# Who subtracts the expert weights: from VectorE and GpSimd in turn to VectorE alone, with the output copy on ScalarE

## The chip, the cores and the metric

The kernel runs on one core of a Trainium2 chip. The metric is the device time of one execution in microseconds. A core has TensorE (PE in the profile), VectorE (DVE), ScalarE (ACT), GpSimd (POOL) and SyncE (SP), which here only issues DMAs. The engines run their own lists of instructions and wait for each other through semaphores.

## What is computed

A transformer block (attention, short convolution, experts, a gated embedding) and then a second one (retention, a Fourier branch, a convolutional feed-forward net), on 512 tokens of 1024 numbers in float32. The change touches the experts of the first block alone:

```python
ht = h.reshape(b * s, d)                       # 512 tokens x 1024
g_val, g_idx = lax.top_k(softmax(ht @ w_rg + b_rg), 1)       # one group of 4 experts
e_val, e_idx = lax.top_k(softmax(e_logits of that group), 2) # two experts in it
a = jnp.einsum('td,edf->tef', ht, w_gate)      # 16 experts, 1024 -> 256
u = jnp.einsum('td,edf->tef', ht, w_up)
hid = jax.nn.silu(a) * u * combine[..., None]
out = jnp.einsum('tef,efd->td', hid, w_down)   # 256 -> 1024
```

Each token goes to 2 of 16 experts: 1024 pairs of a token and an expert.

## The kernel before

**Slots and steps.** The pairs are sorted on the chip into 23 slots of at most 128 pairs: one for each of 16 experts, and 7 more for what overflows. One slot is one step `n`. A step gathers the rows of its tokens from `h_rows` in device memory into `hg` (one indirect DMA, two buffers), transposes them on TensorE, multiplies by the gate and up weights, applies SiLU and the share of the pair (`hid`), transposes `hid`, multiplies by the down weights, copies the result from PSUM to `y_sb` (one buffer) and scatters its rows to `y_rows` (one indirect DMA). Both indirect DMAs are issued by GpSimd.

**Units.** The weights of a step are three units of 1 MB: `3n-1` (gate and up, first half), `3n` (second half) and `3n+4` (down); TensorE uses the units in order of their number, so the down product of step `n-1`, unit `3n+1`, follows the second gate and up unit of step `n`. Products keep float32 precision by splitting every operand in two: ScalarE rounds the unit (`unit_hi`, line 1750), another engine subtracts that from the raw unit (`unit_lo`, line 1755), and TensorE multiplies high by high, high by low and low by high: 12 matmuls of 128x512 a unit, 36 a step. There are four raw buffers and four pairs of split buffers. SyncE loads unit `u` (two DMAs of 512 KB, line 1654) once unit `u-4` is subtracted. ScalarE rounds unit `u` once it has landed and TensorE has used unit `u-4`. Tokens (`s_hi`, `s_lo`, lines 1870 and 1908) and `hid` (`g_hi`, `g_lo`, lines 1888 and 1933) are split in the same way by ScalarE and VectorE.

**Order.** Nothing is planned at run time: each engine's order is its program. In step `n`:

- TensorE: gate and up, first half; transpose `hid` of `n-1` (line 1810); transpose the tokens of `n+1` (line 1775); gate and up, second half; down product of `n-1` (lines 1826 to 1828).
- ScalarE: SiLU (line 1882), round unit `3n+4`, round unit `3n+5`, `g_hi`, tokens of `n+2`, round unit `3n+6`.
- VectorE: `hid` (line 1926), unit `3n+4` if it is VectorE's, copy of the output of `n-1` (line 1913), unit `3n+5`, `g_lo`, tokens of `n+2`, unit `3n+6`.
- GpSimd: gather for step `n+2` (line 1700), scatter of the output of `n-1` (line 1705), unit `3n+4` (line 1755).

GpSimd subtracts the 21 down units of steps 0 to 20 (`POOL_UNITS`), VectorE the other 48. The two count in semaphores of their own, `e_plo` and `e_dlo`, and `wait_unit_lo` picks the one to wait for. The copy of the output waits for the down product of its step (`e_used`) and for the landing of the scatter before it (`e_ystore`); the down product waits for the copy before it (`e_ycopy`). Twice the stage does something else: in step 6 VectorE computes `last_pick` (into `p_lo`, line 1939), and SyncE, after the loads of step 8, waits for it and loads 1 MB of context into the same memory (`ctx_in`, line 1689).

Of the kernel before, what the change touches and what calls it, by code (L numbers as in the profile page):

```python
# [24 lines left out]
ACT = mybir.ActivationFunctionType  # L25
# [69 lines left out]
STEPS = SLOTS  # L95
UNITS = 3 * STEPS
# [66 lines left out]
def build(nc, a, const, out):  # L163
# [7 lines left out]
    with root:  # L171
# [118 lines left out]
        with ExitStack() as s:  # L290
            sb = buffers(s)
            y_sb = sb("y_sb", [P, D])
# [92 lines left out]
        psum = root.enter_context(nc.psum_tensor("psum", [P, 8, T], F32))  # L385
# [1021 lines left out]
        def copy_embedded(act, c):  # L1407
# [2 lines left out]


        E = semaphores("e_wr", "e_matched", "e_chain", "e_shift", "e_exp", "e_routed", "e_hot", "e_stored",
                       "e_hg0", "e_hg1", "e_in0", "e_in1", "e_in2", "e_in3", "e_whi", "e_dlo", "e_plo", "e_used",
                       "e_turned", "e_hi", "e_lo", "e_silu", "e_hid", "e_ycopy", "e_ystore")
        CHOSEN, PLACED, COMBINED, WEIGHED, TABLED, LAST_PICKED = 1, 2, 3, 4, 5, 6
        MATCHED, RANKED, LISTED, SHARED = KC + 1, KC + 2, KC + 3, KC + 4
# [202 lines left out]
        def unit_down(n):  # L1619
            return min(3 * n + 4, UNITS - 1)  # L1620

        POOL_UNITS = [unit_down(n) for n in range(STEPS - 2)]
        DVE_UNITS = [u for u in range(UNITS) if u not in POOL_UNITS]

        def wait_unit_lo(eng, u):
            if u in POOL_UNITS:
                eng.wait_ge(E["e_plo"], POOL_UNITS.index(u) + 1)
            else:
                eng.wait_ge(E["e_dlo"], DVE_UNITS.index(u) + 1)

        def tokens_of(s):

# [59 lines left out]
        def moe_gpsimd(pool):  # L1692
            pool.wait_ge(G["chunk_done"], 2 * (G_WO + 3) + 2)
            for j in range(2):
                pool.memset(hg[j][:, :], 0.0).then_inc(W["wm_silu"], 1)

            def gather(s):
                if s >= 2:
                    pool.wait_ge(E["e_turned"], tokens_turned(s - 2))
                pool.indirect_dma_start(hg[s % 2][:, :], None, h_rows,  # L1700
                                        bass.IndirectOffsetOnAxis(ap=at_row[:, 0, s:s + 1], axis=0),
                                        bounds_check=T - 1, oob_is_err=False).then_inc(E[f"e_hg{s % 2}"], 16)

            def store_y(s):
                pool.indirect_dma_start(y_rows, bass.IndirectOffsetOnAxis(ap=at_row[:, 1, s:s + 1], axis=0),
                                        y_sb[:, :], None, bounds_check=PAIRS - 1, oob_is_err=False)\
                    .then_inc(E["e_ystore"], 16)

            pool.wait_ge(E["e_stored"], 32)
            pool.wait_ge(E["e_routed"], PLACED)  # L1710
            pool.wait_ge(W["wm_silu"], 5)
            for s in range(2):
                gather(s)
            pool.memset(y_sb[:, :], 0.0).then_inc(W["wm_silu"], 1)
            pool.wait_ge(W["wm_silu"], 6)
            store_y(SLOTS - 1)
            for n in range(STEPS):
                if n + 2 < SLOTS:
                    gather(n + 2)
                if n:  # L1720
                    pool.wait_ge(E["e_ycopy"], n)
                    store_y(n - 1)
                if unit_down(n) in POOL_UNITS:
                    unit_lo(pool, unit_down(n))
            pool.wait_ge(E["e_ystore"], 16 * SLOTS)
            wait_unit_lo(pool, UNITS - 1)
            pool.wait_ge(E["e_turned"], tokens_turned(SLOTS - 1))
            from_rows = y_rows.rearrange("(j i p) d -> p j i d", j=TOP, p=P)
            for half in range(2):
                for j in range(TOP):  # L1730
                    pool.dma_start(y_back[:, j, :, half * T:(half + 1) * T], from_rows[:, j, :, half * T:(half + 1) * T])\
                        .then_inc(E[f"e_hg{half}"], 16)
# [8 lines left out]
        def unit_hi(act, u):  # L1741
            if u >= UNITS:
                return
            b = u % 4
            act.wait_ge(E[f"e_in{b}"], 32 * (u // 4) + 32)
            if u >= 4:
                act.wait_ge(E["e_used"], u - 3)
            elif u % 2:
                act.wait_ge(G["chunk_done"], 2 * (G_WO + 3 + u // 2) + 2)
            act.activation(u_hi[b][:, :, :], raw_of(u)[:, :, :], ACT.Copy).then_inc(E["e_whi"], 1)  # L1750

        def unit_lo(eng, u):
            b = u % 4
            eng.wait_ge(E["e_whi"], u + 1)
            eng.tensor_tensor(u_lo[b][:, :, :], raw_of(u)[:, :, :], u_hi[b][:, :, :].bitcast(F32), ALU.subtract)\  # L1755
               .then_inc(E["e_plo" if u in POOL_UNITS else "e_dlo"], 1)

        def pick_bank(c):
            return (6, 7, 0, 1, 2, 3, 6, 7)[c]
# [104 lines left out]
        def moe_scalar(act):  # L1864

            def tokens_hi(s):
                if s == 1:
                    wait_unit_lo(act, 0)
                act.wait_ge(E["e_turned"], tokens_turned(s))
                act.activation(s_hi[s % 2][:, :, :], tokens_of(s), ACT.Copy).then_inc(E["e_hi"], 1)  # L1870

            tokens_hi(0)
            unit_hi(act, 1)
            unit_hi(act, 2)
            tokens_hi(1)
            unit_hi(act, 3)
            act.wait_ge(E["e_stored"], 32)
            for n in range(STEPS):
                act.wait_ge(E["e_used"], unit_in(n, 1) + 1)
                if n >= 2:  # L1880
                    act.wait_ge(E["e_hid"], n - 1)
                act.activation(act_u[:, n % 2, :], psum[:, n % 2, 0:2 * P], ACT.Silu).then_inc(E["e_silu"], 1)
                unit_hi(act, 3 * n + 4)
                unit_hi(act, 3 * n + 5)
                act.wait_ge(E["e_turned"], hidden_turned(n))
                if n >= 2:
                    act.wait_ge(E["e_used"], unit_down(n - 2) + 1)
                act.activation(g_hi[:, n % 2, :, :], psum[:, HID_BANK + n % 2, 0:2 * P].rearrange("p (j t) -> p j t", j=2),
                               ACT.Copy).then_inc(E["e_hi"], 1)
                if n + 2 < SLOTS:  # L1890
                    tokens_hi(n + 2)
                unit_hi(act, 3 * n + 6)
            act.wait_ge(E["e_used"], UNITS)
            act.activation(flat(s_hi[(SLOTS - 2) % 2]).rearrange("p (b t) -> p b t", b=2), psum[:, Y_BANK:Y_BANK + 2, :],
                           ACT.Copy).then_inc(E["e_hi"], 1)
            split_hi(act, G_PG, G_PG % 2)
            for c in range(KC):
                square(act, R_MOE, c)

        def moe_vector(dve):  # L1900

            def dve_lo(u):
                if u in DVE_UNITS:
                    unit_lo(dve, u)

            def tokens_lo(s):
                dve.wait_ge(E["e_hi"], tokens_turned(s))
                dve.tensor_tensor(s_lo[s % 2][:, :, :], tokens_of(s), s_hi[s % 2][:, :, :].bitcast(F32), ALU.subtract).then_inc(E["e_lo"], 1)

            def copy_y(n):  # L1910
                dve.wait_ge(E["e_used"], unit_down(n) + 1)
                dve.wait_ge(E["e_ystore"], 16 * n + 16)
                dve.tensor_copy(y_sb[:, :].rearrange("p (b t) -> p b t", b=2), psum[:, Y_BANK:Y_BANK + 2, :])\
                   .then_inc(E["e_ycopy"], 1)

            tokens_lo(0)
            route_late(dve)
            dve_lo(1)
            dve_lo(2)
            tokens_lo(1)  # L1920
            dve_lo(3)
            for n in range(STEPS):
                dve.wait_ge(E["e_silu"], n + 1)
                if n >= 2:
                    dve.wait_ge(E["e_turned"], hidden_turned(n - 2))
                dve.scalar_tensor_tensor(out=hid[:, n % 2, :], in0=psum[:, n % 2, 2 * P:4 * P], scalar=comb_s[:, n:n + 1],
                                         in1=act_u[:, n % 2, :], op0=ALU.mult, op1=ALU.mult).then_inc(E["e_hid"], 1)
                dve_lo(3 * n + 4)
                if n:
                    copy_y(n - 1)  # L1930
                dve_lo(3 * n + 5)
                dve.wait_ge(E["e_hi"], hidden_turned(n))
                dve.tensor_tensor(g_lo[:, n % 2, :, :], psum[:, HID_BANK + n % 2, 0:2 * P].rearrange("p (j t) -> p j t", j=2),
                                  g_hi[:, n % 2, :, :].bitcast(F32), ALU.subtract).then_inc(E["e_lo"], 1)
                if n + 2 < SLOTS:
                    tokens_lo(n + 2)
                if n == 6:
                    dve.wait_ge(E["e_wr"], 96)
                    dve.tensor_scalar(last_pick, tokens[:, :], last_row[:, 0:1], None, ALU.is_equal).then_inc(E["e_routed"], 1)
                dve_lo(3 * n + 6)  # L1940

            dve.wait_ge(E["e_hi"], LAST)
            mine = (SLOTS - 2) % 2
# [951 lines left out]
```

## Time and profile before

| | |
|---|---|
| time, median of 3 runs | 1792.19 us (1786.09 to 1794.49) |
| the profiled execution, its own time | 1787.65 us |
| its span in the trace | 1785.8 us |
| busy over the span: PE, PEld, DVE, ACT, POOL | 93%, 73%, 51%, 42%, 13% |
| expert steps, first to last `hid` | 484.54 to 790.93 us |

The profile's page slices the span in 40 and gives the busy tenths of each engine; in slices 12 to 18, the expert steps, PE stands at 6 to 8 tenths where it is at 9 nearly everywhere else, the PE clock at 8 to 9 tenths of full speed, and POOL at 5 to 6 where it otherwise has next to nothing. PEld is TensorE's loading of weights, which overlaps the matmuls. "Idle before, releaser" is the time in which an engine stood still ahead of an instruction, and what ended it; it costs nothing unless that engine is what the others wait for. SPq and POOLq are the issuing of DMAs.

### The profile page before, as it was taken

Reading aid. Unit: us, or ns where it says so; the run is one execution under the profiler, and the core shown is the slowest. Engines: PE = TensorE matmul, PEld = TensorE weight load, DVE = VectorE, ACT = ScalarE, POOL = GpSimd, SP = SyncE. Lnnn points to the kernel's source line nnn. Section 1 sums busy time; section 2 is a strip of 40 time slices with the busy share of each in tenths; the row PEclk is TensorE's granted clock in tenths of the full one; section 3 lists DMA queues with packets and bytes.
Section 4 is the critical chain, followed back from the end, with each engine's and each line's share of the span. In section 5 each row is a group of like instructions: output and inputs, shape, how many; then the busy total and the mean of one; then the engine's idle time right before and its main releaser. Section 6 shows DMA issues by size and latency. Waiting matters only on the chain.

```text
span 1785.8 us, 19917 instructions
## 1 busy us (share of the span) xinstructions
PE 1657.5 (93%) x7655; PEld 1306.7 (73%) x7655; DVE 914.2 (51%) x1027; ACT 753.4 (42%) x886; POOL 235.8 (13%) x114
## 2 busy tenths in 40 slices
PE   6999999999678677877999999999999999999998
PEld 5777777888566566665778888877688688888886
DVE  5433334444677677668652423421246565465454
ACT  5554544224454454545653333433213443343343
POOL 1101100000266566640010000000000000000000
PEclk8999999999888898898999999999999999999999
DMA  4466562232577767653242112132133233332321
GB/s 138 130 216 205 173 229 74 91 101 95 180 252 253 277 244 263 245 178 113 67 142 71 48 47 70 47 123 69 69 120 94 70 87 104 89 99 94 94 77 65
DMA packets 183424, 232.37 MB, mean 130 GB/s; under 512 B 13819, under 2 KB 154423, under 8 KB 180031
## 3 DMA queue, kind: packets, MB, share of 16 engines
q1 hardware_dynamic: 175647, 218.88, 37.4%
q0 software_dynamic: 7712, 12.60, 2.0%
q8 instruction: 43, 0.70, 0.2%
q14 instruction: 22, 0.18, 0.0%
HBM read 228.80 MB, written 18.37 MB: 138 GB/s over the span
## 4 chain that ended last, share of the span: by engine, by line
PE 76%; DVE 7%; DMA 6%; POOL 4%; ACT 3%; issue 2%; SPq 1%; POOLq 0%; ACTq 0%; DVEq 0%
PE psum L442 19%; PE psum L444 19%; PE psum L443 19%; DMA hg<-h_rows,at_row 4%; POOL w_lo L1755 2%; POOL w_lo_more L1755 2%; PE psum L2562 2%; PE psum L742 1%; DVE pre L521 1%; PE psum L824 1%; DVE w_lo L1755 1%; DMA raw_more<-in_w_up 1%; PE psum L1229 1%; PE psum L1230 1%; PE psum L1231 1%
## 5 line engine op out<-in xcount | busy, mean ns | idle before, releaser
L442 PE MATMUL psum<-h_hi,w_hi 128*128 128x512 f32 x1160 | 466.6, 402 | 7.6 <-DVE w_lo L419 3.2
L444 PE MATMUL psum<-h_hi,w_lo 128*128 128x512 f32 x1160 | 454.2, 392 | 0.0
L443 PE MATMUL psum<-h_lo,w_hi 128*128 128x512 f32 x1160 | 454.0, 391 | 0.0
L419 DVE TENSOR_TENSOR w_lo<-raw,w_hi 128x2048 fp32r<-128x2048 f32 (+2 forms) x99 | 223.7, 2259 | 224.3 <-ACT w_hi L415 224.3
L442 PEld LDWEIGHTS psum<-h_hi,w_hi 128*128 128x128 f32 x1160 | 218.8, 189 | 69.4 <-issue 18.4
L444 PEld LDWEIGHTS psum<-h_hi,w_lo 128*128 128x128 f32 x1160 | 218.9, 189 | 47.1
L443 PEld LDWEIGHTS psum<-h_lo,w_hi 128*128 128x128 f32 x1160 | 219.2, 189 | 46.6 <-issue 3.6
L415 ACT ACTIVATE w_hi<-raw 128x2048 fp32r<-128x2048 f32 (+2 forms) x100 | 187.9, 1879 | 77.3 <-PE psum L444 70.0
L472 ACT ACTIVATE sq<-x 128x512 f32<-128x512 f32 x56 | 35.3, 632 | 159.2 <-DVE x L1342 105.2
L1755 DVE TENSOR_TENSOR w_lo<-raw,w_hi 128x2048 fp32r<-128x2048 f32 x24 | 83.9, 3498 | 24.2 <-ACT w_hi L1750 24.1
L1755 DVE TENSOR_TENSOR w_lo_more<-raw_more,w_hi_more 128x2048 fp32r<-128x2048 f32 x23 | 79.1, 3439 | 25.5 <-ACT w_hi_more L1750 25.4
L1750 ACT ACTIVATE w_hi_more<-raw_more 128x2048 fp32r<-128x2048 f32 x34 | 64.9, 1910 | 51.8 <-DMA raw_more<-in_w_up 39.2
L1750 ACT ACTIVATE w_hi<-raw 128x2048 fp32r<-128x2048 f32 x34 | 64.9, 1910 | 36.1 <-DMA raw<-in_w_up 29.9
L442 PE MATMUL psum<-d_hi,w_hi 128*128 128x512 f32 x176 | 69.3, 394 | 0.0
L443 PE MATMUL psum<-d_lo,w_hi 128*128 128x512 f32 x176 | 69.3, 394 | 0.0
L444 PE MATMUL psum<-d_hi,w_lo 128*128 128x512 f32 x176 | 69.3, 394 | 0.0
L2745 ACT ACTIVATE cv<-psum,vec 128x512 f32<-128x512 f32 x44 | 32.1, 779 | 84.4 <-PE psum L444 84.4
L1700 POOL DMA_INDIRECT hg<-h_rows,at_row x23 | 60.5, 2630 | 37.7 <-issue 33.2
L1775 PE MATMUL psum<-small,hg 128*128 128x128 f32 x184 | 30.8, 320 | 36.7 <-DMA hg<-h_rows,at_row 36.7
L2768 DVE SCALAR_TENSOR_TENSOR cv<-psum,vec,cv 128x511 f32<-128x511 f32 x44 | 32.8, 745 | 54.8 <-ACT cv L2745 54.8
L1755 POOL TENSOR_TENSOR w_lo_more<-raw_more,w_hi_more 128x2048 fp32r<-128x2048 f32 x11 | 54.9, 4990 | 14.0 <-ACT w_hi_more L1750 13.8
L1775 PEld LDWEIGHTS psum<-small,hg 128*128 128x128 f32 x184 | 26.1, 201 | 39.5 <-DMA hg<-h_rows,at_row 39.3
(389 smaller groups left out, 2745.1 us busy)
## 6 DMA issues: line engine op xcount, KB each, us to landing
raw<-in_w_up SPq DMA_DIRECT2D x67, 512.0 KB, 6.4
wm_raw<-in_w_mod SPq DMA_DIRECT2D x24, 1024.0 KB, 5.4
raw<-in_w_in SPq DMA_DIRECT2D x18, 1024.0 KB
raw<-in_w_in SPq DMA_DIRECT2D x33, 512.0 KB
raw_more<-in_w_down SPq DMA_DIRECT2D x24, 512.0 KB, 7.4
raw<-in_w_gate SPq DMA_DIRECT2D x23, 512.0 KB, 4.5
raw_more<-in_w_gate SPq DMA_DIRECT2D x22, 512.0 KB, 5.0
raw_more<-in_w_up SPq DMA_DIRECT2D x22, 512.0 KB, 6.2
```

The source lines that it names most:

```text
L415: act.activation(w_hi[j][:, 0:tiles, :], raw[j][:, 0:tiles, :], ACT.Copy).then_inc(G["hi_ready"], 1)
L419: dve.tensor_tensor(w_lo[j][:, 0:tiles, :], raw[j][:, 0:tiles, :], w_hi[j][:, 0:tiles, :].bitcast(F32), ALU.subtract).then_inc(G["lo_ready ...
L442: pe.matmul(to, w_hi[j][:, tile, :], hi_k, start=(k == 0), stop=False)
L443: pe.matmul(to, w_hi[j][:, tile, :], lo_k, start=False, stop=False)
L444: return pe.matmul(to, w_lo[j][:, tile, :], hi_k, start=False, stop=last)
L472: act.activation(sq[:, c % 2, :], x[:, c, :], ACT.Square).then_inc(G["sq_ready"], 1)
L1700: pool.indirect_dma_start(hg[s % 2][:, :], None, h_rows, bass.IndirectOffsetOnAxis(ap=at_row[:, 0, s:s + 1], axis=0), bounds_check=T - 1, ...
L1750: act.activation(u_hi[b][:, :, :], raw_of(u)[:, :, :], ACT.Copy).then_inc(E["e_whi"], 1)
L1755: eng.tensor_tensor(u_lo[b][:, :, :], raw_of(u)[:, :, :], u_hi[b][:, :, :].bitcast(F32), ALU.subtract)\
L1775: done = pe.transpose(psum[:, b + k // 4, (k % 4) * P:(k % 4 + 1) * P], of_k[:, k, :], ident)
L2562: done = pe.matmul(psum[:, 5 + g % 2, :], fd[:, g, i, part * P:(part + 1) * P], dft_l[:, part, i, :], start=(n == 0), stop=(n == 7))
L2768: dve.scalar_tensor_tensor(out=buf[:, 1:T], in0=bank[:, 0:T - 1], scalar=vec[:, bass.ds(V_CONV2 + col, 1)], in1=buf[:, 1:T], op0=ALU.mult, ...
```

## The change

VectorE subtracts every unit, in the order in which TensorE uses them; ScalarE copies each step's output from PSUM, between the rounding of units `3n+4` and `3n+5`; GpSimd keeps only its two indirect DMAs a step. One semaphore, `e_wlo`, counts the subtracted units. `unit_lo` gets the guard for numbers past the last unit that `unit_hi` has.

```diff
-                       "e_hg0", ..., "e_whi", "e_dlo", "e_plo", "e_used",
+                       "e_hg0", ..., "e_whi", "e_wlo", "e_used",
-        POOL_UNITS = [unit_down(n) for n in range(STEPS - 2)]
-        DVE_UNITS = [u for u in range(UNITS) if u not in POOL_UNITS]
         def wait_unit_lo(eng, u):
-            if u in POOL_UNITS:
-                eng.wait_ge(E["e_plo"], POOL_UNITS.index(u) + 1)
-            else:
-                eng.wait_ge(E["e_dlo"], DVE_UNITS.index(u) + 1)
+            eng.wait_ge(E["e_wlo"], u + 1)
@@ moe_gpsimd, step n
                 if n:
                     pool.wait_ge(E["e_ycopy"], n)
                     store_y(n - 1)
-                if unit_down(n) in POOL_UNITS:
-                    unit_lo(pool, unit_down(n))
@@ moe_scalar
+            def copy_y(n):
+                act.wait_ge(E["e_used"], unit_down(n) + 1)
+                act.wait_ge(E["e_ystore"], 16 * n + 16)
+                act.activation(y_sb[:, :].rearrange("p (b t) -> p b t", b=2), psum[:, Y_BANK:Y_BANK + 2, :], ACT.Copy)\
+                   .then_inc(E["e_ycopy"], 1)
@@ moe_scalar, step n
                 unit_hi(act, 3 * n + 4)
+                if n:
+                    copy_y(n - 1)
                 unit_hi(act, 3 * n + 5)
@@ moe_vector, step n
-                dve_lo(3 * n + 4)
-                if n:
-                    copy_y(n - 1)
-                dve_lo(3 * n + 5)
+                unit_lo(dve, 3 * n + 4)
+                unit_lo(dve, 3 * n + 5)
```

## Rows read from the trace of the kernel before

**Rows 1.** Waits in 480 to 786 us: engine, line, waited for; total, times, longest.

```profile
POOL y_rows L1705 <- DVE y_sb L1913: 114.6, 21, 12.5
SPq L1654 <- POOL w_lo L1755: 85.8, 10, 10.3
SPq L1654 <- POOL w_lo_more L1755: 83.7, 10, 10.2
SPq L1689 <- DVE p_lo L1939: 13.1, 1, 13.1
```

**Rows 2.** Chain of waits, one double step: start us, us, engine or DMA, line.

```profile
602.68 0.56 issue
...
603.42 1.00 POOL y_rows L1705
...
604.45 5.75 POOL w_lo_more L1755
...
610.34 10.95 DMA hg<-h_rows,at_row
...
621.34 1.97 PE psum L1775 x8
...
623.31 0.43 PE psum L1799
...
629.12 0.23 PE psum L1827
...
629.63 1.24 DVE y_sb L1913
```

**Rows 3.** Groups by line, 480 to 786 us: count; busy us, mean ns; idle before.

```profile
L1755 DVE TENSOR_TENSOR w_lo<-raw,w_hi 128x2048 fp32r<-128x2048 f32 x23 | 81.7, 3550 | 24.2 <-ACT w_hi L1750 24.1
L1750 ACT ACTIVATE w_hi<-raw 128x2048 fp32r<-128x2048 f32 x33 | 63.0, 1910 | 36.1 <-DMA raw<-in_w_up 29.9 <-PE psum L1828 6.2
L1908 DVE TENSOR_TENSOR s_lo<-psum,s_hi 128x1024 fp32r<-128x1024 f32 x22 | 26.8, 1218 | 8.6 <-ACT s_hi L1870 8.6
L1870 ACT ACTIVATE s_hi<-psum 128x1024 fp32r<-128x1024 f32 x22 | 22.6, 1027 | 44.3 <-PE psum L1775 44.3
L1882 ACT ACTIVATE act_u<-psum 128x256 f32<-128x256 f32 x22 | 8.5, 385 | 8.6 <-PE psum L1801 8.6
```

**Rows 4.** Order of time: a subtraction alone, then beside GpSimd; GpSimd's two DMAs.

```profile
555.49 2.29 DVE L1755 TENSOR_TENSOR w_lo_more<-raw_more,w_hi_more 128x2048 fp32r<-128x2048 f32 x1 [0.67 <-ACT w_hi_more L1750]
571.97 5.77 DVE L1755 TENSOR_TENSOR w_lo<-raw,w_hi 128x2048 fp32r<-128x2048 f32 x1 [2.76 <-ACT w_hi L1750]
...
555.62 3.04 POOL L1705 DMA_INDIRECT y_rows<-y_sb,at_row  x1 [5.09 <-DVE y_sb L1913]
589.89 1.03 POOL L1700 DMA_INDIRECT hg<-h_rows,at_row  x1 [0.16 <-issue]
610.34 2.91 POOL L1700 DMA_INDIRECT hg<-h_rows,at_row  x1
```

**Rows 5.** Stretches: us; busy (count) of PE, PEld, DVE, ACT, POOL; PEclk; DMA share; GB/s.

```profile
484.54:784.67 300.13, 234.52 (x958) 188.02 (x957) 215.86 (x128) 152.87 (x127) 185.25 (x61) 0.87 0.70 249
626.80:636.80 10.00, 9.71 (x46) 7.62 (x45) 7.22 (x6) 7.23 (x6) 5.12 (x2) 1.00 0.77 293
540.00:600.00 60.00, 44.29 (x181) 35.69 (x180) 39.93 (x25) 28.86 (x24) 34.04 (x12) 0.84 0.80 284
```

**Rows 6.** Issue to landing by line: scatters (L1705), then gathers (L1700), 23 each.

```profile
DMA to landing us min/median/max: 2.1/4.9/8.5
...
DMA to landing us min/median/max: 4.2/9.2/11.2
```

**Rows 7.** Order of time on VectorE: `hid` of steps 0, 21 and 22.

```profile
484.54 0.48 DVE L1926 SCALAR_TENSOR_TENSOR hid<-psum,comb_s,act_u 128x256 f32<-128x256 f32 x1
...
784.67 0.47 DVE L1926 SCALAR_TENSOR_TENSOR hid<-psum,comb_s,act_u 128x256 f32<-128x256 f32 x1
...
790.93 0.47 DVE L1926 SCALAR_TENSOR_TENSOR hid<-psum,comb_s,act_u 128x256 f32<-128x256 f32 x1
```

More of the change, by code:

```diff
@@ L1412, in build @@
         E = semaphores("e_wr", "e_matched", "e_chain", "e_shift", "e_exp", "e_routed", "e_hot", "e_stored",
-                       "e_hg0", "e_hg1", "e_in0", "e_in1", "e_in2", "e_in3", "e_whi", "e_dlo", "e_plo", "e_used",
+                       "e_hg0", "e_hg1", "e_in0", "e_in1", "e_in2", "e_in3", "e_whi", "e_wlo", "e_used",
                        "e_turned", "e_hi", "e_lo", "e_silu", "e_hid", "e_ycopy", "e_ystore")
@@ L1752, in unit_lo @@
         def unit_lo(eng, u):
+            if u >= UNITS:
+                return
             b = u % 4
@@ L1755, in unit_lo @@
             eng.tensor_tensor(u_lo[b][:, :, :], raw_of(u)[:, :, :], u_hi[b][:, :, :].bitcast(F32), ALU.subtract)\
-               .then_inc(E["e_plo" if u in POOL_UNITS else "e_dlo"], 1)
+               .then_inc(E["e_wlo"], 1)
         def pick_bank(c):
@@ L1900, in moe_vector @@
         def moe_vector(dve):
-            def dve_lo(u):
-                if u in DVE_UNITS:
-                    unit_lo(dve, u)
             def tokens_lo(s):
@@ L1908, in tokens_lo @@
                 dve.tensor_tensor(s_lo[s % 2][:, :, :], tokens_of(s), s_hi[s % 2][:, :, :].bitcast(F32), ALU.subtract).then_inc(E["e_lo"], 1)
[L1910 to L1914, printed above, removed]
             tokens_lo(0)
             route_late(dve)
-            dve_lo(1)
-            dve_lo(2)
+            unit_lo(dve, 1)
+            unit_lo(dve, 2)
             tokens_lo(1)
-            dve_lo(3)
+            unit_lo(dve, 3)
             for n in range(STEPS):
@@ L1939, in moe_vector @@
                     dve.tensor_scalar(last_pick, tokens[:, :], last_row[:, 0:1], None, ALU.is_equal).then_inc(E["e_routed"], 1)
-                dve_lo(3 * n + 6)
+                unit_lo(dve, 3 * n + 6)
             dve.wait_ge(E["e_hi"], LAST)
```

## The prediction

> **What bounds the kernel now.** I read the page first: TensorE is over 90% busy except in the expert steps, so the question is what starves it there. The stretches come next. From `hid` of step 0 to `hid` of step 21 are 300.13 us, 21 steps of 14.29 us [rows 5, 7]; TensorE is busy 234.5 us of them at a mean clock of 0.87, GpSimd 185 us, VectorE 216 us, ScalarE 153 us, and the DMA engines at a share of 0.70. Nothing is full on the mean. One stretch of 10.00 us holds exactly the 46 matmuls and transposes of a step (36 + 8 + 2), with TensorE busy for 9.71 us at clock 1.00 [rows 5]: this is the pace of a step when nothing is late, and 4.3 us a step are lost against it.
>
> The list of waits says who is late: SyncE's weight loads waited 169.5 us for GpSimd's subtractions, 20 times, up to 10.3 us each [rows 1]. GpSimd itself waited 114.6 us for VectorE's copies of the output [rows 1]. The chain of waits ties this into one loop of two steps [rows 2]: from the end of a copy, 0.74 us until GpSimd starts the scatter, 1.03 for that, 5.75 for its subtraction, 0.14, then the gather, 10.95 us from issue to landing, 0.05, 1.97 for the transposes of the gathered tokens, 6.32 for 24 matmuls (some at 0.43 us, some at 0.23), and 1.24 for the next copy. Sum 28.19 us for two steps, 14.1 each: the measured pace. The gather lands that late because the subtraction delays its issue and releases a burst of weight loads in the same microsecond, with which it then shares the DMA engines.
>
> GpSimd's subtraction also costs VectorE: a subtraction of VectorE takes 2.29 us alone and 5.77 beside one of GpSimd; the mean of a group of 23 is 3.55 [rows 3, 4].
>
> **Part 1, GpSimd subtracts nothing.** The loop loses 5.75 us. SyncE's 20 waits for GpSimd go [rows 1] and the loads come one unit at a time as VectorE finishes.
>
> **Part 2, VectorE subtracts all 69 units.** A step then costs VectorE 3 x 2.29, 1.22 for the tokens, 0.47 for `hid` and some 0.4 for `g_lo`: 9.0 us, against 215.86 / 21 = 10.3 now [rows 3, 4, 5, 7]. It gets a subtraction more and has less to do, since it no longer stands beside GpSimd's. It stays under TensorE's 9.7. Should the stretching remain in full (3 x 3.55), a step would be 12.7; I take 2.29, as nothing of that size on GpSimd is left.
>
> In order of use, the down unit `3n+4` is subtracted right after `hid(n)`, on ScalarE's rounding (done 2.3 us after SiLU starts), so at about 4.6 us; the down product wants it 9.7 us after SiLU starts. Slack some 5 us.
>
> **Part 3, ScalarE copies.** No copy of this kind runs on ScalarE; the nearest row is its rounding of tokens, also 128x1024 out of PSUM, 1.03 us [rows 3]. Bounds: 1.03 and VectorE's 1.24 [rows 2]. ScalarE's step becomes 3 x 1.91 + 1.03 + 1.03 and twice 0.385, 8.6 us [rows 3]: under 9.7. Behind the copy on ScalarE stand the rounding of `3n+5` (which waits for the same down product anyway), `g_hi` and the tokens. The copy waits for a down product that ends about 2.8 us (12 matmuls of 0.23) after SiLU starts, while ScalarE is busy for 2.3: 0.5 us of waiting. Then copy to 3.8, rounding to 5.7, `g_hi` when `hid` is transposed, about 6.0, tokens to 8.1, rounding to 10.0. So ScalarE comes round in about 10.0 us, just about TensorE's pace: cover with no slack. If it lies bare, the copy costs 1.03 us a step.
>
> The copy also waits for the landing of the scatter before it. Scatter: 0.74 after its copy, then 4.9 us to landing in the median, 8.5 at most [rows 2, 6]. With the copy, 6.7 to 10.3 us; the next copy is due a step later, so ScalarE would seldom wait.
>
> **Part 4, the gather.** Its loop becomes 0.74 + 1.03 + 0.2 + G + 0.05 + 1.0 (transposes at full clock) + 24 x 0.23 + 1.03 = 9.6 us + G for two steps. G was 4.2 to 11.2 us, median 9.2 [rows 6]. The scatter's issue took 3.04 us instead of 1.0 when a subtraction of VectorE had just begun, and a gather's 1.03 with VectorE idle, 2.91 with it busy [rows 4]. VectorE will now mostly be subtracting, so I add up to 2.0 us for the scatter (the gather's wait is in G). Two steps then take from 9.6 + 4.2 = 13.8 to 9.6 + 2.0 + 11.2 = 22.8 us: 6.9 to 11.4 a step. At the median G of 9.2, 9.4.
>
> The Trainium skill has a rule against this change, SBUF — State Buffer, in "SBUF: two separate sides" (the trap that VectorE blocks DMA): while VectorE holds the port pair that it shares with GpSimd, GpSimd can't write descriptors, and DMAs issued from its queue stall. The 3.04 against 1.00 us agrees, though the page speaks there of a mode with two ports and this is an operation with two inputs. By the rule both DMAs of each step would wait for up to one subtraction; that is the upper end just worked out.
>
> **The sum.** A step lies between TensorE's 9.7 and the gather loop's 11.4; I take the middle, 10.6, because every engine sits within about 1 us of TensorE's pace and the DMA engines too: 300.13 us x 249 GB/s are 74.7 MB, 3.56 MB a step, and at 284 / 0.80 = 355 GB/s when always busy [rows 5] that is 10.0 us. Waits of some tenths here and there will not all overlap.
> 21 steps x (14.29 - 10.6) = 77.5 us gained.
> Given back: the last interval was 6.3 us because the weights were long there [rows 7]; at TensorE's pace it is 9.7, -3.4. Once, after step 8, SyncE waits for `last_pick` (13.1 us now [rows 1]), and VectorE computes that between units 23 and 24, where loads 26 and 27 want to go after units 22 and 23; with 1 MB of context ahead of them I take 6 us (ends 0 and 10).
> 77.5 - 9.4 = 68 us. Profiled execution 1787.65 - 68 = 1719.6; the median of the runs was 4.5 above the profiled one. I take 1721.
>
> **Rivals.**
> *The DMA engines bind.* For: over 60 us they were at a share of 0.80 with 284 GB/s [rows 5], and no longer stretch shows more. If 0.80 is what bursts and waits allow, a step is 3.56 / 0.284 = 12.5 us: 21 x 1.8 - 9.4 = 28, 1760. Against: the gaps of today are SyncE waiting for GpSimd, not the engines' own. 0.13.
> *ScalarE's chain lies bare*, the copy 1.03 us longer a step: 11.6 us, 21 x 2.66 - 9.4 = 46.5, 1743. For: the chain of 10.0 us has no slack. Against: the rounding behind it waits for the same product. 0.12.
> *Everything overlaps*: a step at 9.7, 21 x 4.59 - 3.4 = 93, 1697. 0.08.
> *Slower: the scatter's landing holds ScalarE.* Place: `e_ystore` in ScalarE's `copy_y`, in front of two of three roundings; the loop is copy 1.03 + 0.74 + landing L. It decides from L = 12.5 us on, where a step is 14.3. At L = 15 a step is 16.8, 21 x 2.5 + 9.4 = 62 us more, 1854. Against: 8.5 was the most in 23 [rows 6], and with 2.0 for the descriptors it is still only 12.3 a step. 0.04.
> *It does not remove the loop*, G growing by what the subtraction gave up (to 10.95 + 5.75): 14 us a step, within 0.5% (about 9 us, what a measurement of this kernel can tell). The loads would have to be as bunched as now. 0.03.
> My forecast, a step of 9.9 to 11.4: 0.60.
>
> **Numbers.** Forecast's own range 21 x (14.29 - 11.4) - 9.4 = 51 to 21 x 4.4 - 6 = 86: 1704 to 1739. The range for 8 in 10 takes in bare ScalarE and half of the DMA case: 1701 to 1753. Faster by over 0.5%: 0.60 + 0.13 + 0.12 + 0.08 = 0.93; within: 0.03; slower: 0.04.
>
> **What would show it.** Right: 69 subtractions on VectorE near 2.3 us; no SyncE wait for GpSimd; ScalarE copies of 1.0 us; steps of 10 to 11 us with the PE clock near 1.0; a DMA share near 0.9; GpSimd's two DMAs often at 2 to 3 us. Wrong: gathers landing after 11 us with TensorE waiting for them (the loop stands); long idle on ScalarE before the copy released by the scatter; weight rounding waiting for loads with the DMA share at 0.8; TensorE at half clock through whole steps.

## The result, and the profile after

| | before | after |
|---|---|---|
| median of the runs | 1790.08 us (4 runs, 1786.09 to 1794.49) | 1701.78 us (4 runs, 1700.31 to 1713.41) |
| the profiled execution | 1787.65 us | 1700.52 us |
| first to last `hid` | 484.54 to 790.93 us | 483.01 to 704.27 us |
| a step, `hid` 0 to `hid` 21 over 21 | 14.29 us | 10.22 us |

The change makes the kernel faster: ratio 0.952, 95% interval 0.947 to 0.957. It was predicted at 1721 us, 1701 to 1753: the measured median is 19 us below the forecast and 0.8 us inside the range. The expert steps give 306.4 - 221.3 = 85.1 of the 87.0 us by which the span (1785.8, now 1698.8 us) shrank; 1.5 more come from their earlier start.

The stretch of the 21 steps after, with the columns of [rows 5]:

```profile
483.01:697.60 214.59, 202.02 (x955) 165.27 (x954) 180.99 (x129) 170.56 (x147) 67.22 (x39) 0.98 0.96 349
```

TensorE is busy 94% of it at clock 0.98, where it was 78% at 0.87, and the DMA engines are at a share of 0.96 with 349 GB/s, where they were at 0.70 with 249. The waits in 480 to 700 us, then those of SyncE, as in [rows 1]:

```profile
POOL y_rows L1699 <- ACT y_sb L1869: 141.4, 20, 14.6
ACT y_sb L1869 <- DMA y_rows<-y_sb,at_row: 13.3, 9, 3.6
PEld psum L1769 <- DMA hg<-h_rows,at_row: 4.9, 6, 2.8
...
SPq L1648 <- DVE w_lo L1749: 72.1, 30, 5.1
SPq L1648 <- DVE w_lo_more L1749: 71.0, 30, 7.1
SPq L1683 <- DVE p_lo L1929: 8.2, 1, 8.2
```

No load waits for GpSimd any more, and TensorE waits 5 us for gathers in all. The groups by line, 484 to 700 us, to be held against [rows 3]:

```profile
L1749 DVE TENSOR_TENSOR w_lo_more<-raw_more,w_hi_more 128x2048 fp32r<-128x2048 f32 x32 | 73.2, 2288 | 18.3 <-ACT w_hi_more L1742 18.0
...
L1864 ACT ACTIVATE s_hi<-psum 128x1024 fp32r<-128x1024 f32 x21 | 21.5, 1025 | 7.1 <-PE psum L1769 6.8
L1869 ACT ACTIVATE y_sb<-psum 128x1024 f32<-128x1024 f32 x21 | 21.5, 1024 | 17.5 <-DMA y_rows<-y_sb,at_row 13.3 <-PE psum L1822 4.1
```

VectorE's subtraction has a mean of 2.288 us, where it was 3.55, and ScalarE's copy takes the 1.02 us of the row it was priced by. Issue to landing of scatters and of gathers, as in [rows 6]:

```profile
DMA to landing us min/median/max: 2.1/7.5/10.5
...
DMA to landing us min/median/max: 4.3/8.4/11.0
```

The scatter now takes 2.6 us longer to land in the median, with the DMA engines at a share of 0.96 and not 0.70; this is the cost that the gain brought with it.

### The profile page after: what moved, and what is told of

The parts are those of the page before. It is cut to its first block, busy times and chain, and to the rows that moved or that the text cites. A ratio compares the mean times of both kernels' runs of the same rounds, so it can differ in the third digit from the quotient of the medians.

```text
span 1698.8 us, 19917 instructions
## 1 busy us (share of the span) xinstructions
PE 1623.7 (96%) x7655; PEld 1283.5 (76%) x7655; DVE 877.0 (52%) x1026; ACT 772.6 (45%) x908; POOL 117.8 (7%) x93
## 4 chain that ended last, share of the span: by engine, by line
PE 85%; DVE 5%; ACT 4%; DMA 4%; issue 2%; POOL 0%; SPq 0%; POOLq 0%; ACTq 0%; DVEq 0%
PE psum L442 20%; PE psum L444 20%; PE psum L443 20%; DMA hg<-h_rows,at_row 2%; PE psum L1793 2%; PE psum L1794 2%; PE psum L1795 2%; PE psum L2552 2%; PE psum L742 1%; PE psum L1820 1%; PE psum L824 1%; PE psum L1769 1%; PE psum L1822 1%; PE psum L1821 1%; DMA y_rows<-y_sb,at_row 1%
## 5 line engine op out<-in xcount | busy, mean ns | idle before, releaser
L1749 DVE TENSOR_TENSOR w_lo<-raw,w_hi 128x2048 fp32r<-128x2048 f32 x34 | 77.7, 2286 | 15.9 <-ACT w_hi L1742 15.6
L1694 POOL DMA_INDIRECT hg<-h_rows,at_row x23 | 47.1, 2050 | 48.1 <-issue 36.6
L1342 DVE SCALAR_TENSOR_TENSOR x<-psum,mod,x 128x512 f32<-128x512 f32 x32 | 23.3, 750 | 51.9 <-PE psum L444 51.9
L483 DVE TENSOR_TENSOR ss<-ss,sq 128x512 f32<-128x512 f32 x49 | 33.8, 691 | 11.9 <-ACT sq L472 10.2
L1699 POOL DMA_INDIRECT y_rows<-y_sb,at_row x23 | 28.5, 1240 | 155.5 <-ACT y_sb L1869 148.8
```

The costliest lines, as they stand in the source:

```text
L1694: pool.indirect_dma_start(hg[s % 2][:, :], None, h_rows, bass.IndirectOffsetOnAxis(ap=at_row[:, 0, s:s + 1], axis=0), bounds_check=T - 1, ...
```

## The experiments

All steps below are `hid` 0 to `hid` 21 over 21, from the profiled execution. The medians carry one disturbance that has nothing to do with the change: where TensorE's clock falls early in the router, ahead of the experts, all that follows comes up to 12 us later (shown in the last section). So a difference of 10 us between two medians is read from the steps. A step is not free of noise either: the changed kernel, e7, e8 and e11, whose medians agree within 1.2 us, have steps of 10.10 to 10.22 us, so a tenth of a microsecond between two of them says nothing.

| kernel | us, median (all runs) | a step, us |
|---|---|---|
| before | 1788 to 1792 | 14.29 |
| after | 1701.78 | 10.22 |
| e1 copy back on VectorE | 1727.84 (1717.52 to 1730.22) | 10.96 |
| e2 copy alone to ScalarE | 1803.10 (1797.24 to 1812.42) | 14.96 |
| e3 before, gather ahead of the subtraction | 1811.58 (1811.36 to 1818.37) | 15.27 |
| e9 before, subtraction ahead of the scatter | 1747.08 (1741.38 to 1755.46) | 12.24 |
| e4 after + 2 subtractions between scatter and gather | 1766.28 (1763.52 to 1766.76) | 13.16 |
| e5 after + 2 subtractions behind the gather | 1748.31 (1742.54 to 1754.47) | 12.08 |
| e10 after + 1 subtraction behind the gather | 1723.33 (1718.79 to 1730.85) | 10.92 |
| e11 after + 4 memsets behind the gather | 1702.19 (1701.40 to 1711.04) | 10.18 |
| e6 after, half of the loads | 1696.08 (1695.18 to 1705.19) | 9.75 |
| e7 after, context later | 1701.85 (1701.48 to 1702.16) | 10.10 |
| e8 after, two output buffers | 1702.94 (1701.56 to 1708.84) | 10.15 |
| e12 after, e7 + e8 + earlier gather | 1701.79 (1694.35 to 1708.16) | 10.04 |

**e1: all of the change but ScalarE's copy.**

```diff
 # moe_vector of the changed kernel (and copy_y taken out of moe_scalar)
                 unit_lo(dve, 3 * n + 4)
+                if n:
+                    copy_y(n - 1)
                 unit_lo(dve, 3 * n + 5)
```

> The changed kernel, but VectorE still copies each step's output, where it did before; GpSimd subtracts nothing. The loop theory (GpSimd's subtraction between scatter and gather made the gather late): the gain is almost all there, since only 1.2 us a step moves back to VectorE, 9.0 + 1.2 = 10.2 us against steps of 10.2 us now; about 1705 us, at most 1715. The rival that ScalarE's copy was needed: VectorE becomes the bound with its waits at 11.3 us a step or more, 1725 us or more.

10.96 us a step, 0.74 more than with the change, so 16 us of the 26 between the medians. In the profiled execution `hid` 0 comes 12.3 us later, in the router; the fastest runs of the two, 1717.52 and 1700.31, are 17 us apart, which fits the steps. The expectation took VectorE's 10.2 us of work for its pace and left out what the copy waits for. VectorE in order of time:

```profile
642.18 2.28 DVE L1749 TENSOR_TENSOR w_lo<-raw,w_hi 128x2048 fp32r<-128x2048 f32 x1
645.42 1.23 DVE L1903 COPY y_sb<-psum 128x1024 f32<-128x1024 f32 x1 [0.96 <-DMA y_rows<-y_sb,at_row]
646.56 2.28 DVE L1749 TENSOR_TENSOR w_lo_more<-raw_more,w_hi_more 128x2048 fp32r<-128x2048 f32 x1
```

The copy stands for 0.96 us for the scatter, with a subtraction behind it, and then takes 1.23 us of an engine that has 10.2 us to do. Part of the gain is the copy's, more than the loop theory allowed.

**e2: ScalarE's copy alone, in the kernel before.**

```diff
 # moe_scalar of the kernel before (and copy_y taken out of moe_vector)
                 unit_hi(act, 3 * n + 4)
+                if n:
+                    copy_y(n - 1)
                 unit_hi(act, 3 * n + 5)
```

> The kernel before, with only the output copy moved to ScalarE; GpSimd still subtracts its 21 units. Loop theory: the loop loses 1.24 - 1.03 us of copy in two steps, 2 to 5 us in all, about 1787 us. The rival that VectorE's load was the bound: 1.2 us less a step there, 25 us faster, about 1765 us.

Slower by 0.8%: ratio 1.0079 (1.0050 to 1.0108). Both theories said faster. The same edit is worth +14 us here and, with GpSimd's subtraction gone, -16 (e1 against the change, by steps). The chain of one step, start and duration, and then VectorE and GpSimd in order of time:

```profile
636.84 1.91 ACT w_hi L1750
...
638.78 3.93 DVE w_lo L1755
...
645.47 0.42 DVE g_lo L1933
...
645.98 0.77 PE psum L1826
...
650.42 0.02 ACT y_sb L1875
```

```profile
638.78 6.77 DVE L1755 TENSOR_TENSOR w_lo<-raw,w_hi 128x2048 fp32r<-128x2048 f32 x1 [3.85 <-ACT w_hi L1750]
...
638.77 4.62 POOL L1755 TENSOR_TENSOR w_lo_more<-raw_more,w_hi_more 128x2048 fp32r<-128x2048 f32 x1
```

ScalarE's rounding of `3n+5` is now tied to the copy, and so is GpSimd's scatter; the two paths from the start of the copy, 2.86 us each, arrive within 0.01 us of each other. GpSimd comes first; the 6.77 us of VectorE are GpSimd's 4.62 and then 2.2 of its own. `g_lo` stands behind it on VectorE, the down product waits for `g_lo` and, after the idle time, runs its first matmuls at half clock (0.43 us each, the last 0.23), and the next copy waits for that: 0.92 + 1.91 + 6.77 + 0.42 + 4.44 = 14.5 us from copy to copy, with no gather in it.

**e3: only the gather's place, in the kernel before.**

```diff
 # moe_gpsimd, step n (gather(2) stands ahead of the loop)
-                if n + 2 < SLOTS:
-                    gather(n + 2)
                 if n:
                     pool.wait_ge(E["e_ycopy"], n)
                     store_y(n - 1)
+                if n + 3 < SLOTS:
+                    gather(n + 3)
                 if unit_down(n) in POOL_UNITS:
                     unit_lo(pool, unit_down(n))
```

> The kernel before, with GpSimd issuing the next gather between its scatter and its subtraction, not after it. Loop theory in its narrow form (only the gather's issue was late): 5.9 us leave the loop of 28.2 and the gather goes ahead of the burst of loads, steps of about 11.5 to 12.5 us, 1735 to 1755 us. The rival that the loads were late because they wait for GpSimd's subtraction: no more than 15 us faster, 1775 us or more. The rival that the two engines' subtractions stretching each other was the cost: the same, 1775 us or more.

Slower by 1.3%: ratio 1.0126 (1.0082 to 1.0170). My loop through the gather, as the prediction told it, falls as the sole bound. The chain of a step:

```profile
562.83 1.24 DVE y_sb L1914
...
564.86 1.03 POOL y_rows L1705
...
566.18 1.89 POOL hg L1700
568.10 4.56 POOL w_lo L1756
572.79 0.77 PE psum L1827
...
577.20 1.24 DVE y_sb L1914
```

From copy to copy are 14.4 us, in one step: copy, scatter, gather's issue, subtraction of the down unit, down product (its matmuls 0.43 us apart, TensorE having stood idle for it), copy. This loop of one step was in the kernel before too, without the 1.89. There, in the step that follows the copy at 601.39 us, in order of time:

```profile
604.45 5.75 POOL L1755 TENSOR_TENSOR w_lo_more<-raw_more,w_hi_more 128x2048 fp32r<-128x2048 f32 x1
...
610.34 0.47 PE L1826 MATMUL psum<-w_hi_more,g_hi 128*128 128x512 f32 x1 [2.36 <-POOL w_lo_more L1755]
...
614.96 1.23 DVE L1913 COPY y_sb<-psum 128x1024 f32<-128x1024 f32 x1 [2.22 <-PE psum L1828]
```

Copy to copy 13.57 us in one step, against 28.2 us for two through the gather [rows 2]: nearly the same pace, and the chain shows whichever ended last. Taking the subtraction out of the longer one leaves the other in front, and here lengthened it by the gather's issue.

That is not all of e3. The next step took 16.5 us, from the copy at 577.20 to that at 593.67, and shows a third path, through the weight loads. SyncE's waits for GpSimd in 484 to 700 us, then ScalarE's rounding and VectorE's subtraction in that step:

```profile
SPq L1654 <- POOL w_lo L1756: 75.3, 7, 12.3
SPq L1654 <- POOL w_lo_more L1756: 59.4, 6, 12.8
...
579.34 1.91 ACT L1751 ACTIVATE w_hi<-raw 128x2048 fp32r<-128x2048 f32 x1 [7.70 <-DMA raw<-in_w_up]
...
581.28 7.05 DVE L1756 TENSOR_TENSOR w_lo<-raw,w_hi 128x2048 fp32r<-128x2048 f32 x1 [2.85 <-ACT w_hi L1751]
```

The loads wait for GpSimd's subtraction, which now comes behind the gather's issue: 134.7 us in 13 waits, 10.4 each, where it was 8.5 each (169.5 in 20, [rows 1]). ScalarE waits 7.70 us for the weights, VectorE's subtraction takes 7.05 us beside one of GpSimd's, and `g_lo`, down product and copy stand behind it. The rival of late loads, which the expectation named, fits e3 as well as the loop of one step; e3 does not tell them apart.

**e9: before, subtraction first.** Who subtracts and who copies is as before.

```diff
 # moe_gpsimd, step n (gather(2) stands ahead of the loop)
-                if n + 2 < SLOTS:
-                    gather(n + 2)
+                if unit_down(n) in POOL_UNITS:
+                    unit_lo(pool, unit_down(n))
                 if n:
                     pool.wait_ge(E["e_ycopy"], n)
                     store_y(n - 1)
+                if n + 3 < SLOTS:
+                    gather(n + 3)
-                if unit_down(n) in POOL_UNITS:
-                    unit_lo(pool, unit_down(n))
```

> The kernel before, with GpSimd doing its subtraction of unit 3n+4 first, then the scatter and the next gather; who subtracts and who copies is unchanged. Second theory, from the run with the gather first: the bound before was a loop of ONE step, copy of the output, scatter, GpSimd's subtraction of the down unit, down product, next copy (1.24 + 0.74 + 1.0 + 4.6 to 5.8 + 12 matmuls at 0.23 to 0.43, with the gather tied to it every second step). This order cuts it, as the subtraction no longer waits for the copy: steps of 11.5 to 12.5 us, 1730 to 1755 us. The rival that the two engines' subtractions excluding each other were the whole cost: no gain, 1780 us or more.

1747 us, 0.975 (0.972 to 0.978); 12.24 us a step, as expected. Both loops are shorter by the subtraction, and the loads wait for GpSimd 3.9 us each time and not 8.5 (69.6 us in 18 waits), so this run too leaves open how much was which. But 2.05 of the 4.07 us a step are a matter of order on GpSimd's list, and need no other engine. The rest is not: VectorE's subtractions have a mean of 2.74 to 2.82 us here and GpSimd's scatter takes 2.4 to issue.

**e4 and e5: the changed kernel, with GpSimd's time put back and nothing else.** Two subtractions of 128x1024 a step into memory that is free there; no engine waits for them. In e4 they stand between scatter and gather, in e5 the next gather goes ahead of them.

```diff
 # moe_gpsimd, step n (e5: gather(n + 2) is gone from its head, gather(2) stands ahead of the loop)
                     store_y(n - 1)
+                if n + 3 < SLOTS:          # e5 only
+                    gather(n + 3)
+                if n < STEPS - 2:
+                    for half in range(2):
+                        pool.wait_ge(E["e_side"], 2 * n + half)
+                        pool.tensor_tensor(sq[...], small[:, 0:1, :].to_broadcast([P, 8, P]),
+                                           small[:, 1:2, :].to_broadcast([P, 8, P]), ALU.subtract).then_inc(E["e_side"], 1)
```

> The changed kernel, with 21 times two subtractions of 128x1024 added on GpSimd for which nobody else waits (about 4.6 us together), where its subtraction stood: between scatter and gather. Loop theory: 9.6 + 4.7 + a gather of 9 to 11 us are 23.5 to 25.5 us for two steps, 11.8 to 12.8 each, 33 to 54 us slower than the change: 1735 to 1756 us. If the shared time of VectorE and GpSimd is the cost, VectorE has 9.0 + 4.6 = 13.6 us a step and the time is 1770 us; if only the waiting of the loads for GpSimd was, nothing is lost here: 1702 us.

> The changed kernel with the same added subtractions on GpSimd, nobody waiting for them, but the next gather is issued ahead of them. The loop as such is whole again, and VectorE's subtractions still meet GpSimd's. Loop theory: near the changed kernel, at most 15 us slower, 1702 to 1717 us. The rival that the shared time of VectorE and GpSimd was the cost: VectorE 13.6 us a step, 1770 us. Between them if both count.

e4 gives back 2.94 us a step, e5 1.86. So with no other engine waiting for these results and the gather ahead of them, GpSimd's subtractions cost 39 us (46 by the medians); the place ahead of the gather costs another 23. The narrow loop theory allowed e5 15 us. In neither run does a weight load wait for GpSimd, so the late loads were not the whole cost before: without them 2.94 of the 4.07 us a step are back in e4, though with two subtractions that take 6.2 us there (3.12 each), where the one before took 5.0. GpSimd and VectorE in e5, in order of time:

```profile
617.71 6.81 POOL L1714 TENSOR_TENSOR sq<-small 128x1024 f32<-128x1024 f32 x2
624.68 2.88 POOL L1699 DMA_INDIRECT y_rows<-y_sb,at_row  x1 [0.15 <-issue]
627.87 1.90 POOL L1694 DMA_INDIRECT hg<-h_rows,at_row  x1 [0.30 <-issue]
...
618.18 4.11 DVE L1759 TENSOR_TENSOR w_lo_more<-raw_more,w_hi_more 128x2048 fp32r<-128x2048 f32 x1
622.21 0.47 DVE L1928 SCALAR_TENSOR_TENSOR hid<-psum,comb_s,act_u 128x256 f32<-128x256 f32 x1
622.61 4.07 DVE L1759 TENSOR_TENSOR w_lo<-raw,w_hi 128x2048 fp32r<-128x2048 f32 x1
```

The durations are those of two engines that take turns: the shortest small subtraction of this run takes 2.35 us, and 2.35 + 2.28 + 2.35 are 7.0 us, near the 6.81 that two take GpSimd here, while two of VectorE's take 4.1 each instead of 2.29; GpSimd's list of a step, with the stretched issue of its DMAs, is 6.8 + 2.9 + 1.9 + 0.5 = 12.1 us: the step. It is GpSimd's own list that binds, not VectorE's 13.6 us as the rival had it.

**e10: one such subtraction, e11: memsets in its place.** e10 is e5 with `range(1)`; e11:

```diff
+                    for part in range(4):
+                        pool.wait_ge(E["e_side"], 4 * n + part)
+                        pool.memset(sq[:, :, :], 0.0).then_inc(E["e_side"], 1)
```

> The changed kernel with one added subtraction of 128x1024 on GpSimd a step behind the gather, not two (with two: 1748 us, steps of 12.1 us, in which GpSimd is never idle). If it was GpSimd's own list that bound there (6.8 + 2.9 + 1.9 us and small gaps), it falls to 8.7 us and does not bind; VectorE is held up for 1.8 us once, 10.8 us a step: about 1715 us. If the price is linear in the time that GpSimd holds: 1725 us.

> The changed kernel with four memsets of 128x1024 on GpSimd a step behind the gather (3.9 us together), in place of the two added subtractions: GpSimd writes as much time away but reads nothing. If GpSimd and VectorE exclude each other only where GpSimd reads SBUF: VectorE's subtractions stay at 2.29 us and the time near 1702 us. If any instruction of GpSimd counts: VectorE's at 3.3 us in the mean and 1740 to 1750 us.

e10: 10.92 us a step, 0.70 more than without, against 1.86 for two: not linear, since GpSimd's list does not bind at one. e11: 10.18 us a step with 3.8 us of memsets on GpSimd in each (80.7 / 21). The groups of e11, 484 to 700 us:

```profile
L1714 POOL MEMSET sq<- 128x1024 f32 x84 | 80.7, 961 | 3.6
L1758 DVE TENSOR_TENSOR w_lo<-raw,w_hi 128x2048 fp32r<-128x2048 f32 x32 | 73.2, 2288 | 13.2 <-ACT w_hi L1751 12.8
```

Memsets, which write SBUF (the on-chip memory) but read nothing, run beside VectorE's subtractions and stretch neither: all 84 take 0.95 to 0.98 us, and VectorE's mean is 2.288 us as in the changed kernel. The Trainium skill, SBUF — State Buffer, "SBUF: two separate sides", says this: a VectorE operation with two inputs in SBUF holds the shared pair of ports only against a GpSimd operation that reads SBUF. Both runs agree: in e10, where GpSimd reads, VectorE's means are 2.74 and 2.81 us. So the cost of e5 is the meeting of the two engines and not GpSimd's time as such.

**e6, e7, e8, e12: what bounds the changed kernel.**

```diff
 # e6, moe_sync (half of each unit from unit 5 on keeps old numbers; its one DMA counts for two)
-                for i, src in enumerate(pieces):
+                for i, src in enumerate(pieces if u < 5 else pieces[:1]):
 # e7
-                if n == 8:
+                if n == 11:
                     sp.wait_ge(E["e_routed"], LAST_PICKED)
 # e8: two buffers, a semaphore each
-                act.wait_ge(E["e_ystore"], 16 * n + 16)
+                if n != 1:
+                    act.wait_ge(E[f"e_ystore{n % 2}"], 16 * (n // 2) + 16 * (1 - n % 2))
-                act.activation(y_sb[:, :]...
+                act.activation(y_sb[:, n % 2, :]...
 # e12: e7, e8, and in moe_gpsimd gather(n + 3) ahead of the wait for copy n - 1
```

> The changed kernel, with only the first of the two 512 KB DMAs of each weight unit from unit 5 on (the second half of a unit keeps old numbers), so 1.05 + 0.37 MB less the half: some 2.0 instead of 3.5 MB a step. If the DMA engines bind the changed kernel (share 0.98 to 0.99 in its middle): steps fall from 10.2 to TensorE's 9.5 to 9.7, 10 to 15 us faster, the context's stall shrinks too: about 1688 us. If TensorE and ScalarE's chain bind it: no more than 5 us.

> The changed kernel, with SyncE waiting for last_pick and loading the context after the loads of step 11, not step 8. My prediction gave this one stall 6 us; in the trace the three steps around it take 11.2, 14.2 and 11.3 us, 7 more than three others. Expected: the wait for last_pick is gone and 4 to 7 us with it, about 1696 us. If the 1 MB of context is the cost and not the wait, it only moves: no change.

> The changed kernel with two buffers for the output copy, so that ScalarE does not wait for the landing of the scatter just before. In the trace that wait is 13.3 us, 9 times, on ScalarE ahead of the copy. If it is on the path: some 5 to 10 us faster, about 1694 us. If TensorE's pace and the DMA engines cover it: no change, 1702 us.

> A try at a faster version: the changed kernel with two output buffers, the context load after step 11, and GpSimd issuing the next gather before it waits for the copy. One by one the first two gave nothing. TensorE's own pace is 9.46 us a step (seen with half of the loads), the changed kernel's 10.2: if waits for gather, scatter and context add up to the difference, 10 us faster, 1692 us; if the DMA engines (share 0.98 to 0.99) hold it, no change, 1700 us.

With half of the loads, TensorE is never idle in the late steps of e6 (the columns of [rows 5]):

```profile
600.00:700.00 100.00, 100.00 (x485) 83.35 (x485) 91.71 (x66) 86.63 (x75) 38.39 (x20) 1.00 0.61 197
```

and its last 12 steps take 9.46 us each: the pace of TensorE's 46 matmuls and transposes when it is never idle and at full clock. The changed kernel is 0.76 above it on the mean, 16 us in 21 steps: 4.0 in the first six, 8.3 in the three around the context load (11.2, 14.2 and 11.3 us), 3.7 in the last twelve. With half of the data 0.47 a step go, 9.8 us in all (5.7 by the medians, 5.1 by the fastest runs), most of it in the first six and the last twelve; the three steps around the context still lose 6.9. In e7 SyncE's wait for `last_pick`, 8.2 us before, is gone, and the long step has moved with the load (13.2 us, between `hid` 10 and 11): it is the 1 MB, or what it does to the loads behind it, and not that wait. The second output buffer is worth nothing measurable, although ScalarE's 13.3 us of waiting for scatters stood in the list: they were covered. e12's 21 steps are 3.7 us shorter in all and its fastest run is the fastest of any kernel, 1694.35 us, but its median is the changed kernel's; whether it is faster is not settled.

## Why the prediction was right, and where it was not

1. *GpSimd's subtraction is what starves TensorE.* Right: taking it off the other engines' way is 3.33 of the 4.07 us a step (e1). *Through the one loop of two steps.* Incomplete: e3 cut that loop and the time rose. There was a second loop of nearly the same length, and this one of a single step (copy, scatter, subtraction of the down unit, down product) is not in the prediction. Its parts were: 1.24 + 0.74 + 1.0 + 5.75, and the down product. A third path, the loads that wait for the subtraction, is named there but has no time of its own; how much was this path and how much the loop of one step, no run tells. I read the chain of waits over one double step and took what ended last for all that bound. The forecast came out all the same because its sum does not use the old loop's length: it adds up what is left, and all three paths go with the same instruction. That part is luck.
2. *Engines excluding each other.* Priced well (2.29 us a subtraction after, predicted 2.29), but I treated it as VectorE's busy time alone. e5 shows that it is worth 1.86 us a step without any wait between the engines, through both lists (e11, with nearly as much time of GpSimd and no meeting, costs nothing), and that the scatter's issue stretches with it, to 2.9 us in the steps shown.
3. *ScalarE's copy*: 1.02 us against 1.03 predicted, hidden as predicted: e6 has it on ScalarE too and steps of 9.46 us. That it gains 0.74 us a step (e1) I had not counted, and alone it loses (e2).
4. *The sum.* Predicted gain 68 us of the profiled execution, measured 87.1. The terms: a step of 10.6 was 10.22 (8.0 us); that stall, 6 us, was counted on top although 10.22 holds it; the last interval was 6.67 us and not 9.7, since `hid` 21 stands behind a subtraction on VectorE and `hid` 22 behind none, after as before (3.0 us); the steps began 1.5 us earlier. Together 18.5 of 19.0. The term that was mis-sized is the plain step, 10.6 us: the 18 steps away from the context load took 9.88 us. The upper bound of 11.4, the gather's loop at its latest landing, never held: gathers landed after 8.4 us in the median and TensorE waited 4.9 us for them in all. The step lies between two other figures of the prediction, TensorE's 9.7 (9.46 in e6) and the DMA engines' 10.0. The stall at the context load was given 6 us and took 8.3. The 355 GB/s behind the 10.0 fit long stretches (351 and 360 GB/s over 40 us, at shares of 0.99 and 0.98) but are no ceiling: from 560 to 580 us, around the context load, the engines moved 383 GB/s. And 1719.6 + 4.5 would have been 1724, not 1721; the median after is 1.3 us above the profiled execution.
5. *The rivals.* The DMA engines at 0.80: no, the holes were SyncE's waits, and the share rose to 0.96. The scatter holding ScalarE: it happens, 9 times and 13.3 us in all, 7.5 us to landing in the median instead of 4.9, and is covered (e8). ScalarE's chain bare: no (e6). The forecast's own case, a step of 9.9 to 11.4 us, is what came; its time of 1704 to 1739 missed by 2 us.

## What to carry to other kernels

- Before pricing what leaves a loop, list every loop that goes through the same instruction and add each of them up. A chain of waits shows the one that ended last; a second of nearly the same length can stand right behind it (e3), and a helper engine's list is where both are tied together. The cheap edit is to put the work that waits for nothing ahead of the work that waits (e9: 41 us for a reordering).
- An engine that works for you for free may not be free: two engines that hold each other up cost on both lists, though no semaphore connects them (e5). Compare the same instruction's duration alone and in company.
- The worth of moving an instruction depends on what else has been moved: the copy to ScalarE cost 14 us before and gained 16 after.

## What the runs showed of the hardware that I had not expected

Ahead of the experts, in the router (which picks the experts), TensorE's clock falls to the lower level, 1.2 GHz, in every profiled execution, but not at the same place, though the instructions are the same. The stretch from 430 to 455 us, changed kernel first, then e1 (which differs only after this stretch):

```profile
430.00:455.00 25.00, 23.24 (x155) 20.26 (x154) 12.66 (x40) 13.38 (x23) 0.00 (x0) 0.94 0.43 150
```

```profile
430.00:455.00 25.00, 24.19 (x125) 22.17 (x123) 6.25 (x10) 12.25 (x20) 1.36 (x2) 0.71 0.12 43
```

In the changed kernel the clock falls at about 452 us, when the router's eight groups of transposes and small products are done. In e1 it falls at about 440.6, in the third group (mean clock 0.71, so the lower level for more than half of the stretch):

```profile
439.38 0.63 PE L1444 MATMUL psum<-small,h 128*128 128x128 f32 x4
439.85 1.01 PE L1447 MATMUL psum<-wr_raw,h 128*128 128x20 f32 x8
440.70 1.10 PE L1444 MATMUL psum<-small,h 128*128 128x128 f32 x4
441.58 1.74 PE L1447 MATMUL psum<-wr_raw,h 128*128 128x20 f32 x8
```

Eight small products then take 1.74 us instead of 0.97, and `hid` of step 0 comes at 495.3 us instead of 483.0. The other executions fit: where the clock falls between about 440 and 443 us (e1, e6, e9, e12), `hid` 0 comes at 494.2 to 495.4 us; where it falls at 446 us or later, at 483.0 to 488.3. TensorE had been busy almost without a pause before it fell in e1 (0.81 us idle in 430 to 440 us), so the clock did not fall for lack of work there; what sets the place is open. This is the likeliest reason for runs of one kernel that lie 10 to 13 us apart: of the four runs of the changed kernel the one at 1713.41 us has a mean clock of 0.977 over its span, the others, 1700.31 to 1703.05 us, 0.982 to 0.984.
